# Two-block layer: stick-breaking attention summed by parts, and chunked attention's bias and maximum in one operation

## The chip, the cores and the metric

One core of one Trainium2 chip runs the program. The metric is the device time of one execution in microseconds (us). All data are float32. In the profile PE is TensorE (PEld its weight loads), DVE is VectorE, ACT is ScalarE, POOL is GpSimd and SP is the queue that issues weight loads.

## What is computed

The kernel computes two transformer blocks on 1024 rows of width 1024. Only a part of the second block is touched here: its two attentions, each with 8 heads of width 64.

```python
def chunked_attention(...):        # branch 0: a band of 9 chunks of 64 keys
    scores = einsum(q, k) * dh ** -0.5
    scores = where(valid, scores + bias, -inf)
    probs = softmax(scores, axis=-1)
    out = einsum(probs, v)

def stick_breaking_attention(q, k, v):   # branch 1: all keys before the query
    z = einsum(q, k) * dh ** -0.5
    log_keep = where(causal, -softplus(z), 0.0)
    log_after = cumsum(log_keep, reverse=True) - log_keep
    w = where(causal, exp(log_sigmoid(z) + log_after), 0.0)
    out = einsum(w, v)
```

In branch 1, softplus and log_sigmoid are never taken: keep = sigmoid(-z), take = sigmoid(z), left[j] is the product of keep from key j to the last key, and w[j] = take[j] * left[j+1].

## The kernel before, in words

The program is written out by hand for each engine: one Python function per engine and stage issues that engine's instructions in a fixed order, and semaphores (`mark` and `at`) tie the engines together. An engine never passes an instruction that waits. There is no scheduler.

The stage that matters is `att2`, from about 2075 to 2365 us. It has 64 units of work, `UNITS`: units 0 to 31 are branch 0 (4 pairs of heads, 8 query blocks of 128 rows each, t = 0 to 7) and units 32 to 63 are branch 1 (4 pairs, query blocks in the order t = 6, 7, 4, 5, 2, 3, 0, 1). A unit has two heads (hh = 0 and 1). In branch 0 a unit has 128 to 640 keys, in branch 1 it has 128 * (t + 1). Two units make a group g, whose values are summed at once. Every engine loops over u; in step u

- PE (`pe_att2`): scores of unit u + 2 (L3447, for branch 1 then the causal mask, L3456), the turning of unit u's weights, 128 x 128 blocks through PSUM banks 4 and 5 in turn (L3469), and half of the value sums of an earlier group (L3486). Scores over 512 keys take both PSUM banks of their head, so the next unit's scores must wait until all readers of them are done.
- ACT (`act_att2`): branch 0: exp with the maximum as bias (L3526); branch 1: keep (L3531) and take (L3533) from PSUM, for unit u + 2, head 0 before the copying of unit u's turned blocks to SBUF (L3544) and head 1 behind it. It also copies the output's high half (L3560).
- DVE (`dve_att2`): branch 0: scores plus bias (L3602), then their maximum (L3604), for unit u + 2; 1/sum (L3613); the output's scaling (L3639). Branch 1: the running product `left` of unit u + 1 (L3626), the copying of every second turned block group (L3635), and the output's low half (L3646). In branch 0 ACT copies all turned blocks.
- POOL (`pool_att2`): loads queries (L3681), keys and values of the next pair of heads (L3251, L3252; the values go to `v2`, as 8 blocks of 128 keys), biases; in branch 1 it multiplies take by the shifted left into w (L3702), which PE then turns.

`E2` has 6 slots of 1024 columns, a slot for each head of three units. `Sc` has 6 such slots too. Its first five are also `B`, the bias of branch 0; in branch 1 they hold take and w. In the first 6 units of branch 1 the scan's unused second operand is the scanned tile itself (SBUF), from then on a PSUM column.

Of the kernel before, what the change touches and what calls it, by code (L numbers as in the profile page):

```python
# [3420 lines left out]
def value_sums(g):  # L3421

    br, p, t = UNITS[2 * g]
    kbs = range(max(0, t - 4) if br == 0 else 0, t + 2)
    cols = {kb: slice(128 if kb > t else 0, 128 if br == 0 and kb == t - 4 else 256) for kb in kbs}
    return [(kb, cols[kb]) for kb in [t] + [kb for kb in kbs if kb != t]]


def pe_att2(k, e, free):
# [6 lines left out]
    def scores(u):  # L3436
# [5 lines left out]
        for a in range(0, n, 512):  # L3442
            w = min(512, n - a)
            for hh in range(2):
# [4 lines left out]
                free[b] = [s.dve.at("biased", u, hh) if br == 0 else s.act.at("take", u, hh)]  # L3449
# [64 lines left out]
def act_att2(k, e):  # L3514
    s, PS, H = k.att2, k.PS, k.H
    st, E, Sc = k.st2, k.E2, k.Sc

    def exponents(u, hh):
        br, p, t = UNITS[u]
        n, sl = span(br, t)[1], slot(u, hh)  # L3520
        if br == 0:
# [4 lines left out]
            e.activation(ev, ev, ACT.Exp, bias=st[:, sl, 0:1], accum_out=st[:, sl, 1:2]).then_inc(*s.act.mark("exp", u, hh))  # L3526
# [692 lines left out]
```

## Time and profile before

| | |
|---|---|
| median of 3 runs | 3213.13 us |
| lowest and highest run | 3210.9 and 3216.05 us |
| the profiled execution's own time | 3212.68 us |
| its span in the trace | 3210.8 us |
| PE, DVE, ACT, POOL busy, share of the span | 96%, 72%, 41%, 25% |

The profile shows the profiled execution alone. "Busy" counts every moment in which an instruction of the engine is shown; PE's ends are modelled and overlap, so its busy time is more than its work. Waits name who was waited for and for how long in all. A line such as L3604 is a line of the kernel before.

### The profile page before, as it was taken

How to read it: one execution, taken by the hardware profiler on the slowest of the kernel's cores; microseconds unless marked ns; L12 is line 12 of the kernel's file. 1: busy time of each engine (PE TensorE's matmuls, PEld its weight loads, DVE VectorE, ACT ScalarE, POOL GpSimd, SP SyncE). 2: the span in 40 equal slices, each digit the busy share in tenths (PEclk: the TensorE clock that was granted, in tenths of full speed). 3: DMA queues.
4: the chain of work that ended last, by engine and by line, in shares of the span. 5: the costliest groups of instructions: out<-in, count | busy, mean ns of one | idle time of the engine just before them, and what ended most of it. 6: DMA issues, size and time to landing. Idle time of an engine off the chain costs nothing.

```text
span 3210.8 us, 37676 instructions
## 1 busy us (share of the span) xinstructions
PE 3082.9 (96%) x14546; PEld 2417.3 (75%) x14546; DVE 2305.5 (72%) x3084; ACT 1303.1 (41%) x2124; POOL 807.8 (25%) x831
## 2 busy tenths in 40 slices
PE   7999998999999899999999999998899989999999
PEld 3577876777887788888877888764567877888787
DVE  6654456975657977778888566686644699899896
ACT  5431114761134433344454323476632344444443
POOL 1211101321120443320002444313533124333101
PEclk9999999999999999999999999999999999999999
DMA  6433352206743222246343346521123422222823
GB/s 223 156 133 132 136 206 102 80 14 236 266 142 116 99 86 86 80 150 226 112 135 112 97 124 202 174 99 39 39 89 113 156 86 85 79 85 73 298 89 112
DMA packets 118299, 406.86 MB, mean 127 GB/s; under 512 B 13704, under 2 KB 16328, under 8 KB 113642
## 3 DMA queue, kind: packets, MB, share of 16 engines
q1 hardware_dynamic: 65626, 200.42, 19.7%
q0 software_dynamic: 52496, 204.04, 17.7%
q8 instruction: 116, 1.90, 0.2%
q14 instruction: 61, 0.50, 0.0%
HBM read 321.50 MB, written 82.90 MB: 126 GB/s over the span
## 4 chain that ended last, share of the span: by engine, by line
PE 80%; DVE 11%; issue 3%; ACT 3%; DMA 2%; POOL 1%; SPq 0%; ACTq 0%; DVEq 0%; POOLq 0%
PE PS L455 23%; PE PS L457 23%; PE PS L456 23%; PE PS L1255 2%; PE PS L1295 2%; DVE HL L411 2%; PE PS L3447 2%; PE PS L1285 1%; PE PS L3469 1%; DMA RAW<-in_w_whyp 1%; POOL Sc L3702 1%; PE PS L3486 1%; ACT HL L393 1%; DVE Xp L1110 1%; DVE H L750 0%
## 5 line engine op out<-in xcount | busy, mean ns | idle before, releaser
L455 PE MATMUL PS<-H,HL 128*128 128x512 f32 x1920 | 761.1, 396 | 14.5 <-DVE H L3754 7.2
L456 PE MATMUL PS<-H,HL 128*128 128x512 f32 x1920 | 752.1, 392 | 0.0
L457 PE MATMUL PS<-H,HL 128*128 128x512 f32 x1920 | 752.0, 392 | 0.0
L393 ACT ACTIVATE HL<-RAW 128x512 fp32r<-128x512 f32 (+1 forms) x429 | 312.0, 728 | 619.6 <-PE PS L457 562.0
L411 DVE TENSOR_TENSOR HL<-RAW,HL 128x512 fp32r<-128x512 f32 (+1 forms) x429 | 400.1, 933 | 145.2 <-ACT HL L393 135.8
L455 PEld LDWEIGHTS PS<-H,HL 128*128 128x128 f32 x1920 | 363.2, 189 | 104.1 <-issue 19.3
L456 PEld LDWEIGHTS PS<-H,HL 128*128 128x128 f32 x1920 | 363.3, 189 | 76.9 <-issue 2.6
L457 PEld LDWEIGHTS PS<-H,HL 128*128 128x128 f32 x1920 | 363.1, 189 | 76.8
L455 PE MATMUL PS<-HT,HL 128*128 128x512 f32 x720 | 282.5, 392 | 17.8 <-DVE rows L2410 15.7
L456 PE MATMUL PS<-HT,HL 128*128 128x512 f32 x720 | 281.6, 391 | 0.0
L457 PE MATMUL PS<-HT,HL 128*128 128x512 f32 x720 | 281.4, 391 | 0.0
L393 ACT ACTIVATE HL<-SX 128x512 fp32r<-128x512 f32 x180 | 112.9, 629 | 247.5 <-PE PS L457 236.9
L455 PE MATMUL PS<-hsr,HL 128*128 128x512 f32 x464 | 182.1, 392 | 5.9 <-DVE hsr L2524 5.9
L456 PE MATMUL PS<-hsr,HL 128*128 128x512 f32 x464 | 181.3, 391 | 0.0
L457 PE MATMUL PS<-hsr,HL 128*128 128x512 f32 x464 | 181.2, 391 | 0.0
L455 PEld LDWEIGHTS PS<-HT,HL 128*128 128x128 f32 x720 | 136.1, 189 | 49.3 <-DVE HL L411 17.2
L457 PEld LDWEIGHTS PS<-HT,HL 128*128 128x128 f32 x720 | 136.0, 189 | 28.4
L456 PEld LDWEIGHTS PS<-HT,HL 128*128 128x128 f32 x720 | 136.2, 189 | 28.2
L411 DVE TENSOR_TENSOR HL<-SX,HL 128x512 fp32r<-128x512 f32 x180 | 134.5, 749 | 5.2 <-ACT HL L393 2.2
L328 POOL TENSOR_TENSOR SX<-RAW 128x512 f32<-128x512 f32 x56 | 73.8, 1319 | 243.6 <-DVE HL L411 205.9
L335 POOL TENSOR_TENSOR SX<-RAW,SX 128x512 f32<-128x512 f32 x56 | 105.1, 1877 | 96.4 <-DVE HL L411 96.4
L3447 PE MATMUL PS<-k,q 64*128 64x128 f32 (+3 forms) x384 | 95.3, 511 | 16.4 <-ACT Sc L3533 13.6
(465 smaller groups left out, 5633.0 us busy)
## 6 DMA issues: line engine op xcount, KB each, us to landing
RAW<-in_w_up SPq DMA_DIRECT2D x100, 512.0 KB, 3.6
RAW<-in_w_down SPq DMA_DIRECT2D x82, 512.0 KB, 3.8
RAW<-in_w_proj SPq DMA_DIRECT2D x48, 512.0 KB, 3.6
scr_hid<-hidr POOLq DMA_DIRECT2D x36, 512.0 KB, 2.9
RAW<-in_w_wmodr SPq DMA_DIRECT2D x32, 512.0 KB, 4.5
HL<-in_w_dfwd POOLq DMA_DIRECT2D x16, 1024.0 KB, 6.8
HL<-in_w_dinv POOLq DMA_DIRECT2D x16, 1024.0 KB, 5.4
RAW<-in_w_wout SPq DMA_DIRECT2D x26, 512.0 KB, 4.4
```

Of the source, the lines that this page charges most:

```text
L328: e.tensor_tensor(SX[:, 0, :], b[:, 0:512], b[:, 512:1024], ALU.add).then_inc(*signal.mark(j, "s1"))
L335: e.tensor_tensor(SX[:, 2, :], a[:, 512:1024], SX[:, 1, :], ALU.subtract).then_inc(*signal.mark(j, "s4"))
L393: e.activation(part_slot(k, p)[0], src, ACT.Copy).then_inc(*k.high.mark(j, x))
L411: e.tensor_tensor(lo, part_source(k, j, x)[0], hi.bitcast(F32), ALU.subtract).then_inc(*k.low.mark(j, x))
L455: e.matmul(out, lh, rh, start=first, stop=False, skip_group_check=goes_on)
L456: e.matmul(out, lh, rl, start=False, stop=False, skip_group_check=goes_on)
L457: return e.matmul(out, ll, rh, start=False, stop=last, skip_group_check=goes_on)
L1110: e.scalar_tensor_tensor(a, u, c, a, ALU.mult, ALU.add).then_inc(*s.dve.mark("mod", n))
L1255: x = e.matmul(k.PS[:, 3 * m + c, 0:b - a], k.q1[r, h % 2, blk(t)], k.k1[r, h % 2, a:b], start=True, stop=True)
L1285: x = e.transpose(PS[:, b, at + 128 * q:at + 128 * q + 128], weights_of(k, j, 0)[:, blk(4 * c + q)], k.ident[:, :])
L1295: x = e.matmul(PS[:, 7, 0:128], k.WT1[:, j % 2, kb, :], k.v1[:, j // 8 % 2, kb, :], start=(kb == 0), stop=(kb == 9))
L3447: x = e.matmul(PS[:, b, 0:w], k.q2[r, g % 2, blk(t % 2)], k.k2[r, pn % 2, lo * 128 + a:lo * 128 + a + w], start=True, stop=br == 0 or a + ...
```

## The change

1. **Branch 0, DVE.** The addition of the bias and the maximum are one operation, `tensor_tensor_reduce`, with -1 as a factor: E holds -(scores + bias), the reduction is a minimum, and ACT's exp takes scale -1. It is two instructions in the program, the operation and a read of its accumulator.
2. **Branch 0, copies.** Of a unit's turned block groups every second one is copied by DVE, as in branch 1 before.
3. **Branch 1, by parts.** take and w are gone. Since w[j] = left[j+1] - left[j], the output is the last row of v plus the sum over j of left[j] * (v[j-1] - v[j]). PE turns left out of `E2` at once. ACT makes only keep. POOL multiplies nothing.
4. **Branch 1, the steps of v.** For each pair of heads POOL sets one row to 0 (`load_steps`) and loads the values once more, shifted by one key: 127 partitions in one DMA, the 7 rows of partition 0 in another. DVE (`steps`) subtracts v from it in place (1024 columns) and then, in v's own place, adds v at partition 127 alone to the difference. This happens in step u = 30, 38, 46 and 54, ahead of the low half and the scans; the loads are issued in POOL's step u = 26, 34, 42 and 50, behind the keys and values of that pair. The place of the steps is slot 5 of `Sc`, or slot 0.
5. **Branch 1, value sums.** The diagonal key block's sum over 256 columns becomes two over 128, one with the changed v and one with the steps. All others take the steps. PE waits for `steps` ahead of the sums.
6. A bank of scores in branch 1 is free at keep, in branch 0 at the maximum.

```diff
-                unit.append((heads, c, w, 4 + n % 2, "dve" if br and len(unit) % 2 else "act"))
+                unit.append((heads, c, w, 4 + n % 2, "dve" if len(unit) % 2 else "act"))
...
 def value_sums(g):
...
+    if br:
+        left, right = slice(0, 128), slice(128, 256)
+        if t == 0:
+            return [(0, left, True, True, True), (0, right, False, True, False), (1, right, True, False, True)]
+        return ([(kb, slice(0, 256), False, kb == 0, False) for kb in range(t)]
+                + [(t, left, True, False, True), (t, right, False, False, False), (t + 1, right, True, False, True)])
...
+def v_steps(k, p):
+    return k.Sc[:, 5 * (1 - p % 2), :].rearrange("p (t n) -> p t n", t=8)
...
-                free[b] = [s.dve.at("biased", u, hh) if br == 0 else s.act.at("take", u, hh)]
+                free[b] = [s.dve.at("max", u, hh) if br == 0 else s.act.at("keep", u, hh)]
...
-                e.wait_ge(*(s.act.at("exp", u, hh) if br == 0 else s.pool.at("w", u, hh)))
-                src = k.E2 if br == 0 else k.Sc
+                e.wait_ge(*(s.act.at("exp", u, hh) if br == 0 else s.dve.at("left", u, hh)))
...
+            if br:
+                e.wait_ge(*s.dve.at("steps", p, 1))
...
-        for i, (kb, cols) in list(enumerate(sums))[m * half:m + m * half]:
+        for kb, cols, whole, first, last in sums[m:] if half else sums[:m]:
+            v = k.v2[:, pn % 2] if whole else v_steps(k, p)
...
-        e.wait_ge(*s.dve.at("biased", NU // 2 - 1, 1))
-        e.activation(Sc[:, sl, 0:n], z, ACT.Sigmoid).then_inc(*s.act.mark("take", u, hh))
...
-        e.tensor_tensor(ev, scores_of(k, u, hh), B[:, 2 * p + hh, 640 - n:640], ALU.add).then_inc(*s.dve.mark("biased", u, hh))
-        e.wait_ge(*s.dve.at("biased", u, hh))
-        e.tensor_reduce(st[:, sl, 0:1], ev, AX.X, ALU.max, negate=True).then_inc(*s.dve.mark("max", u, hh))
+        e.tensor_tensor_reduce(ev, scores_of(k, u, hh), B[:, 2 * p + hh, 640 - n:640], -1.0, 3.0e38, ALU.add, ALU.min,
+                               st[:, sl, 0:1]).then_inc(*s.dve.mark("max", u, hh))
...
+    def steps(p):
+        v, d = k.v2[:, p % 2], v_steps(k, p)
+        e.wait_ge(*k.in_pair[p % 2].at(4 + p, 1))
+        e.wait_ge(*k.in_steps[p % 2].at(p, 1))
+        e.wait_ge(*s.pool.at("first", p))
+        e.tensor_tensor(d, d, v, ALU.subtract).then_inc(*s.dve.mark("steps", p, 0))
+        e.wait_ge(*s.dve.at("steps", p, 0))
+        e.scalar_tensor_tensor(v, v, k.ident[:, 127:128], d, ALU.mult, ALU.add).then_inc(*s.dve.mark("steps", p, 1))
...
+def load_steps(k, e, p):
+    s, d, src = k.att2, v_steps(k, p), k.d_v2[1][:, :, blk(p)].rearrange("t p n -> p t n")
+    if p == 1:
+        e.wait_ge(*s.dve.at("max", NU // 2 - 1, 1))
+    at = k.in_steps[p % 2]
+    e.memset(d[0:1, 0, :], 0.0).then_inc(*s.pool.mark("first", p))
+    e.dma_start(d[1:128], src[0:127]).then_inc(*at.mark(p, 0))
+    e.dma_start(d[0:1, 1:8], src[127:128, 0:7]).then_inc(*at.mark(p, 1))
...
-        if u + 1 < NU and UNITS[u + 1][0] == 1:
-            n = span(1, UNITS[u + 1][2])[1]
-            for hh in range(2):
-                sl = slot(u + 1, hh)
-                tk = Sc[:, sl, 0:n - 1]
-                e.wait_ge(*s.dve.at("left", u + 1, hh))
-                e.wait_ge(*s.act.at("take", u + 1, hh))
-                e.tensor_tensor(tk, tk, E[:, sl, 1:n], ALU.mult).then_inc(*s.pool.mark("w", u + 1, hh))
+            if u // 8 + 1 >= 4:
+                load_steps(k, e, u // 8 - 3)
```

Where instructions move, three places show it; a tile's name there ends in a number that means nothing (`E_121` is `E2`, `v_119` is `v2`). First ACT, in branch 1, from the last step of one pair of heads to the first long units (896 and 1024 keys) of the next. Before:

```order
L3531 ACTIVATE E_121<-PS 128x896
L3533 ACTIVATE Sc_120<-PS 128x896
L3531 ACTIVATE E_121<-PS 128x1024
L3533 ACTIVATE Sc_120<-PS 128x1024
L3544 ACTIVATE WT_122<-PS 128x2x2x128
L3531 ACTIVATE E_121<-PS 128x1024
L3533 ACTIVATE Sc_120<-PS 128x1024
L3560 ACTIVATE H<-PS 128x256
```

And of the change:

```order
L3544 ACTIVATE E_121<-PS 128x896
L3544 ACTIVATE E_121<-PS 128x1024
L3555 ACTIVATE WT_122<-PS 128x2x2x128
L3544 ACTIVATE E_121<-PS 128x1024
L3571 ACTIVATE H<-PS 128x256
```

Each keep stands alone; the takes into `Sc` behind them are gone, and nothing else has moved on ACT here.

Second DVE in branch 0, one step with 640 keys (`Rb` is the scaled output). Before:

```order
L3602 TENSOR_TENSOR E_121<-PS,Sc_120 128x640
L3604 TENSOR_REDUCE st_127<-E_121 128x1
L3602 TENSOR_TENSOR E_121<-PS,Sc_120 128x640
L3604 TENSOR_REDUCE st_127<-E_121 128x1
L3639 TENSOR_TENSOR Rb_125<-PS,Rb_125 128x256
```

And of the change:

```order
L3613 ISA E_121,st_127<-PS,Sc_120 128x640
L3613 ISA st_127 128x1
L3613 ISA E_121,st_127<-PS,Sc_120 128x640
L3613 ISA st_127 128x1
L3655 COPY WT_122<-PS 128x4x128
L3659 TENSOR_TENSOR Rb_125<-PS,Rb_125 128x256
```

The two reductions have become two short accumulator reads, and a copy that was ACT's stands ahead of the scaling.

Third POOL, from the loads of the next pair of heads on. Before:

```order
L3251 DMA k_118<-scr_qk 128x1024
L3252 DMA v_119<-scr_v 128x8x128
L3702 TENSOR_TENSOR Sc_120<-Sc_120,E_121 128x767 x2
L3702 TENSOR_TENSOR Sc_120<-Sc_120,E_121 128x383 x2
L3681 DMA q_117<-scr_qk 128x256
```

And of the change:

```order
L3251 DMA k_118<-scr_qk 128x1024
L3252 DMA v_119<-scr_v 128x8x128
L3712 MEMSET Sc_120 1x128
L3713 DMA Sc_120<-scr_v 127x8x128
L3714 DMA Sc_120<-scr_v 1x7x128
L3703 DMA q_117<-scr_qk 128x256 x4
```

The multiplications are gone, and POOL's queue holds only loads: three more instructions stand behind the values of each pair.

## Rows read from the trace of the kernel before

**Rows 1.** Stretches: length, PE, PEld, DVE, ACT, POOL busy (instructions), PE clock, DMA share, GB/s.

```profile
2084.84:2185.04 100.20, 99.80 (x745) 61.82 (x745) 86.59 (x203) 77.26 (x204) 13.40 (x23) 1.00 0.29 100
2185.04:2205.05 20.01, 14.84 (x74) 8.48 (x74) 5.12 (x7) 14.84 (x21) 5.66 (x3) 0.74 0.02 7
2205.05:2239.04 33.99, 27.74 (x200) 17.78 (x200) 29.32 (x28) 17.61 (x40) 17.77 (x18) 0.95 0.12 41
2239.04:2251.11 12.07, 8.97 (x44) 4.19 (x44) 5.54 (x5) 8.16 (x11) 4.94 (x5) 0.98 0.06 17
2251.11:2279.61 28.50, 25.74 (x175) 15.93 (x176) 21.07 (x25) 16.78 (x37) 17.62 (x18) 0.95 0.15 50
2279.61:2319.87 40.26, 35.07 (x219) 20.41 (x218) 26.62 (x29) 24.93 (x48) 22.57 (x23) 0.96 0.12 39
2319.87:2357.47 37.60, 31.79 (x208) 18.65 (x207) 25.06 (x26) 24.44 (x47) 19.38 (x18) 1.00 0.03 10
2357.47:2365.20 7.73, 5.96 (x40) 3.74 (x39) 2.44 (x5) 2.13 (x5) 1.65 (x4) 1.00 0.01 2
```

**Rows 2.** Waits, chunked half, 2084.84 to 2185.04 us: total us, times, longest.

```profile
PEld PS L3447 <- DVE E L3602: 6.0, 13, 1.1
...
PEld PS L3469 <- ACT WT L3544: 3.7, 10, 0.4
```

**Rows 3.** Groups of instructions, chunked half, 2075 to 2186 us.

```profile
L3604 DVE TENSOR_REDUCE st<-E 128x1 f32<-128x640 f32 (+4 forms) x64 | 41.8, 654 | 2.2
L3602 DVE TENSOR_TENSOR E<-PS,Sc 128x640 f32<-128x640 f32 (+4 forms) x64 | 41.5, 648 | 1.1 <-PE PS L3447 0.6
```

**Rows 4.** Groups by form, whole run: the fused operation of the first block, line 1463.

```profile
L1463 DVE CUSTOM_DVE_ANT_0 E<-PS,st 128x1280 f32<-128x1280 f32 x54 | 78.7, 1488 | 18.7 <-PE PS L1255 18.7
...
L1463 DVE DVE_READ_ACCUMULATOR2_ANT st<- 128x1 f32 x64 | 5.3, 83 | 0.0
```

**Rows 5.** Groups, one full pair of heads, 2239.04 to 2279.61 us.

```profile
L3626 DVE TENSOR_TENSOR_SCAN E<-E,PS 128x256 f32<-128x256 f32 (+7 forms) x17 | 21.8, 1299 | 0.9 <-ACT E L3531 0.9
...
L3635 DVE COPY WT<-PS 128x512 f32<-128x512 f32 (+1 forms) x8 | 5.2, 644 | 5.2 <-PE PS L3469 5.2
```

**Rows 6.** Timeline, second long unit of a pair: start us, us, instruction.

```profile
2285.29 0.44 PE L3456 MATMUL PS<-maskr,identr 128*128 128x128 f32 x2
...
2285.65 1.02 ACT L3531 ACTIVATE E<-PS 128x1024 f32<-128x1024 f32 x1 [2.33 <-PE PS L3456]
...
2286.57 1.02 ACT L3533 ACTIVATE Sc<-PS 128x1024 f32<-128x1024 f32 x1
2287.47 0.60 ACT L3544 ACTIVATE WT<-PS 128x512 f32<-128x512 f32 x1
...
2288.85 1.06 ACT L3533 ACTIVATE Sc<-PS 128x1024 f32<-128x1024 f32 x1
...
2291.24 0.44 PE L3456 MATMUL PS<-maskr,identr 128*128 128x128 f32 x2
```

**Rows 7.** Groups by form, whole run: scans with and without a PSUM operand.

```profile
L3626 DVE TENSOR_TENSOR_SCAN E<-E 128x1024 f32<-128x1024 f32 x2 | 6.0, 3004 | 0.0
...
L3626 DVE TENSOR_TENSOR_SCAN E<-E,PS 128x1024 f32<-128x1024 f32 x6 | 13.7, 2276 | 0.0
```

**Rows 8.** Groups by form, whole run: VectorE operations like those that are added.

```profile
L411 DVE TENSOR_TENSOR HL<-RAW,HL 128x1024 fp32r<-128x1024 f32 x103 | 132.1, 1284 | 109.4 <-ACT HL L393 102.0 <-ACT acc2r L1932 7.4
...
L2816 DVE SCALAR_TENSOR_TENSOR HTf<-HTf,gsc,RR 128x512 f32<-128x512 f32 x16 | 11.6, 747 | 0.1
L1971 DVE SCALAR_TENSOR_TENSOR HTf<-HTf,gsc,PS 128x512 f32<-128x512 f32 x16 | 11.5, 741 | 1.2 <-PE PS L1920 1.2
```

**Rows 9.** DMA, while a pair's values land, 2263.9 to 2265.4 us: packets; queue's engine share; issues.

```profile
DMA packets 104, 0.37 MB, mean 249 GB/s; under 512 B 13, under 2 KB 13, under 8 KB 104
...
q0 software_dynamic: 104, 0.37, 87.6%
...
v<-scr_v POOLq DMA_DIRECT2D x1, 512.0 KB, 5.7
```

More of the change, by code:

```diff
@@ L3423, in value_sums @@
     br, p, t = UNITS[2 * g]
-    kbs = range(max(0, t - 4) if br == 0 else 0, t + 2)
-    cols = {kb: slice(128 if kb > t else 0, 128 if br == 0 and kb == t - 4 else 256) for kb in kbs}
-    return [(kb, cols[kb]) for kb in [t] + [kb for kb in kbs if kb != t]]
+    if br:
[4 more added lines that the diff above has]
+                + [(t, left, True, False, True), (t, right, False, False, False), (t + 1, right, True, False, True)])
+    kbs = range(max(0, t - 4), t + 2)
+    cols = {kb: slice(128 if kb > t else 0, 128 if kb == t - 4 else 256) for kb in kbs}
+    order = [t] + [kb for kb in kbs if kb != t]
+    return [(kb, cols[kb], True, kb == t, kb == order[-1]) for kb in order]
+def v_steps(k, p):
+    return k.Sc[:, 5 * (1 - p % 2), :].rearrange("p (t n) -> p t n", t=8)
 def pe_att2(k, e, free):
@@ L3465, in turn @@
             for i, hh in enumerate(heads):
-                e.wait_ge(*(s.act.at("exp", u, hh) if br == 0 else s.pool.at("w", u, hh)))
-                src = k.E2 if br == 0 else k.Sc
+                e.wait_ge(*(s.act.at("exp", u, hh) if br == 0 else s.dve.at("left", u, hh)))
                 for q in range(w):
-                    y = e.transpose(PS[:, b, blk(w * i + q)], src[:, slot(u, hh), blk(c + q)], k.ident[:, :])
+                    y = e.transpose(PS[:, b, blk(w * i + q)], k.E2[:, slot(u, hh), blk(c + q)], k.ident[:, :])
             y.then_inc(*s.pe.mark("turn", u, x))
@@ L3481, in values_of @@
                     e.wait_ge(*turned(k, u, x))
+            if br:
+                e.wait_ge(*s.dve.at("steps", p, 1))
             claim(b)
-        for i, (kb, cols) in list(enumerate(sums))[m * half:m + m * half]:
+        for kb, cols, whole, first, last in sums[m:] if half else sums[:m]:
+            v = k.v2[:, pn % 2] if whole else v_steps(k, p)
             for hh in range(2):
                 r = slice(64 * hh, 64 * hh + 64)
-                x = e.matmul(PS[r, b, cols], k.v2[:, pn % 2, kb, r], k.WT2[:, g % 2, hh, kb, cols], start=(i == 0), stop=(i == 2 * m - 1),
-                             skip_group_check=True)
+                x = e.matmul(PS[r, b, cols], v[:, kb, r], k.WT2[:, g % 2, hh, kb, cols], start=first, stop=last, skip_group_check=True)
         if half == 0:
@@ L3515, in act_att2 @@
     s, PS, H = k.att2, k.PS, k.H
-    st, E, Sc = k.st2, k.E2, k.Sc
+    st, E = k.st2, k.E2
     def exponents(u, hh):
@@ L3525, in exponents @@
                 e.wait_ge(*s.dve.at("inv", u - 3))
-            e.activation(ev, ev, ACT.Exp, bias=st[:, sl, 0:1], accum_out=st[:, sl, 1:2]).then_inc(*s.act.mark("exp", u, hh))
+            e.activation(ev, ev, ACT.Exp, bias=st[:, sl, 0:1], scale=-1.0, accum_out=st[:, sl, 1:2]).then_inc(*s.act.mark("exp", u, hh))
             return
@@ L3658, in dve_att2 @@
                 biased(u + 2, hh)
+        if u >= NU // 2 - 2 and u % 8 == 6 and u // 8 - 3 < 4:
+            steps(u // 8 - 3)
         scan = u + 1 < NU and UNITS[u + 1][0] == 1
@@ L3681, in load_queries @@
     e.dma_start(k.q2[:, g % 2, :], k.d_qk2[8 * br + p][:, blk(t // 2, 256)]).then_inc(*k.in_q[g % 2].mark(g))
+def load_steps(k, e, p):
[6 more added lines that the diff above has]
+    e.dma_start(d[0:1, 1:8], src[127:128, 0:7]).then_inc(*at.mark(p, 1))
 def pool_att2(k, e):
-    s, E, Sc = k.att2, k.E2, k.Sc
     for u in range(NU + 2):
@@ L3912, in build @@
         k.in_q = [dma(f"in_q{i}") for i in range(2)]
+        k.in_steps = [dma(f"in_steps{i}") for i in range(2)]
         k.in_gate = [dma(f"in_gate{i}") for i in range(4)]
```

## The prediction

> **What bounds the kernel now.** I first cut the stage in stretches by the moment at which PE first turns a block of a unit, and read who is busy in each [rows 1]. The reader is to see two halves of one stage that have different limits. In the chunked half PE shows 99.8 us of 100.2; DVE (86.6) and ACT (77.3) have little room. In the stick-breaking half (2205 to 2365 us) nobody is full: PE shows 27.7 of 34.0 us, then 34.7 of 40.6 (8.97 and 25.74 of 12.07 and 28.50), and DVE 26.6 of the same 40.6. So the second half is a chain from engine to engine, and what shortens the chain shortens the kernel. What follows the stage starts when it ends, on data that are already there, so I count each microsecond saved in it in full; outside it nothing changes.
>
> Second, the waits of the chunked half: weight loads wait 6.0 us for DVE's additions before scores and 3.7 us for ACT's copies before turning [rows 2]. PE's own row hides these, because its ends overlap.
>
> Third, the timeline where a pair of heads begins, the stretch of 12.07 us [rows 6]. Its unit has 1024 keys, hence both score banks of each head. From mask (2285.29) to mask (2291.24) there are 5.95 us, and they are ACT's: keep, take, a copy, keep, take, and only then PE's next scores. A take costs 0.90 us from its start to the next start (2286.57 to 2287.47).
>
> **The change, part by part.** The sum is made against the profiled execution, 3212.68 us, which is 0.45 us below the median of the runs.
>
> *Chunked half.* Gone from DVE: 64 reductions at 654 ns, 41.8 us [rows 3]. Added: 64 accumulator reads at 83 ns, 5.3 us; the fused operation itself I price from the same operation in the first block, 1280 columns in 1488 ns [rows 4]. At 640 columns that is 0.74 us if it is halved and 0.87 us on the line through the 747 ns that a two-input operation takes at 512 columns [rows 8]; either way it is what an addition costs now (648 ns in the mean over all sizes [rows 3]), so it takes the addition's place at no cost. Added too are 24 copies (one a unit for t = 2 to 7, 4 pairs) at about 644 ns [rows 5], 15.5 us. DVE falls by 41.8 - 5.3 - 15.5 = 21 us, ACT by some 14. But PE shows 99.8 of 100.2 us, so the gain is only what PE waits for. From below it is 0 (PE was full). From above it is twice the 9.7 us of weight-load waits for DVE and ACT [rows 2], since a late head also breaks the pairing of the two heads' scores on PE; but the pairing I can't price, and I cut this at 14. A bank of scores is freed 0.08 us later for head 0 than today, yet some 0.6 us sooner for head 1, which no longer waits for head 0's reduction. I take **-7**.
>
> *The switch between the halves*, 20.0 us with PE at a mean clock of 0.74, that is for a part at 1.2 GHz. ACT is the chain here: two tables swapped, four takes of about 0.9 us before the next scores are in, and two copies. The takes leave (3.6 us) and a copy or two goes to an idle DVE; but PE's own work behind them, partly at the low clock, stays. Ends -1 and -6; I take **-3**.
>
> *First pair of the second half*, 33.99 us, DVE 29.3 busy. Here scans read SBUF twice while POOL multiplies: 1024 columns take 3004 ns against 2276 with a PSUM operand [rows 7]. POOL stops multiplying, so ten scans lose up to 0.73 us each; I take 5 us off DVE, leaving 24, and PE's 27.7 sets the end: **-7** (ends -5 and -8).
>
> *Two full pairs*, 40.57 and 40.26 us. The opening 12.07 us hold two such links; each loses two takes, so 4 x 0.9 = 3.5 us: 8.6 remain. In the other 28.5 us the multiplication on POOL between scan and turning is gone, and the takes too; what is late next is DVE, in order: scan, copy, scan, copy. DVE has 26.6 us a pair and gets the steps: 1.28 us for the subtraction, between 1.28 and 2 x 0.75 us for the other [rows 8], so 2.6, in all 29.2. PE's shown 25.7 of 28.5 has overlaps in it, so I let these 28.5 become 25. Each pair then takes 33.6: **-14** for both. Ends: -8 (the opening links and a little) and -20 (DVE's 29.2 plus one us).
>
> The second operation of the steps reads two SBUF tiles. In this trace such an operation takes 747 ns at 512 columns against 741 with one operand in PSUM [rows 8], so two SBUF inputs cost nothing extra. The Trainium skill says otherwise (Vector Engine (DVE) Microarchitecture Reference, section Points that are easy to get wrong): this form with two SBUF sources that are not bf16 runs at half the throughput. By that rule the sum would be up to 4 us higher; the row decides.
>
> *Last pair*, 37.60 us: the same less the next pair's scores, **-6** (ends -4 and -8). *Tail*, 7.73 us: two waits for POOL's product go, **-0.7**.
>
> *At nothing:* the split of the diagonal value sum (32 matmuls more, each half as wide as the one it replaces, so the same columns); exp's factor; POOL's added issues, which stand in a queue that waits most of the time; the steps' DMA, if it lands like the values, 5.7 us after its issue [rows 9], four steps (about 16 us) ahead of its use. If that cover is gone, DVE stops, with all scans and copies behind it: see the second rival.
>
> Sum: 7 + 3 + 7 + 14 + 6 + 0.7 = 37.7; 3212.7 - 37.7 = **3175**.
>
> **Rivals.**
> 1. *PE is the bound all along.* Its 99.8 of 100.2 us and 34.7 of 40.6 are real work, so only the takes on the chain count. Chunked 0, switch -1, pairs -5, -8, -4: 3212.7 - 18 = 3195. For: PE's rows. Against: it waits for ACT and POOL in the stick half, and its shown ends overlap. Chance 0.12.
> 2. *The shifted load is slow* (the other side). Values land as packets of 4 KB, one a partition: 91 of them and 13 small ones fill 87.6% of 16 engines for 1.5 us, so 0.23 us a packet [rows 9]; 128 over 16 engines are quick. 127 partitions don't divide by 16. If they all go to one DMA engine, that is 127 x 0.23 = 29 us. For pairs 2 to 4 the load is issued just over a microsecond after the first turning of the third unit of the pair before and `steps` is due some 16 us after that turning: DVE would stand 15 to 16 us in each, 47 in all, and at the first pair some 5 more beyond what it idles anyway. 3175 + 52 = 3227. It decides for slower once the stops pass 38 us in all, some 11 a pair. For: no load in this trace has such a shape, so nothing here excludes it. Against: an engine that cuts 127 rows in 8 a piece is as fast as now. Chance 0.13. The Trainium skill (DMA: Bandwidth & Descriptors, section Why a DMA increments its semaphore by 16 and not by 1) states both: the engine count must divide the slowest dimension, so 127 partitions use one, but some direct copies issued from GpSimd are spread over all 16 with 8 partitions each.
> 3. *The fusion does not fuse.* In the first block its second tensor is one broadcast value; with a full bias tile it may need two passes, 1.49 us at 640 columns. DVE keeps its 41.8 us and gets the reads and copies on top, 107 us in the 100-us half: +7 there in place of -7, so 3189. Chance 0.05.
>
> **How the numbers follow.** The forecast (3157 to 3195 with all ends at once) gets 0.66, rival 1 0.12, rival 2 0.13, rival 3 0.05, and 0.04 is for what I don't see, most of it near no change. Some 0.2% (6.4 us) can be told from no change. Faster: 0.66 + 0.12 + 0.05 = 0.83; same 0.03; slower 0.14. The range, 3157 to 3198, takes in the forecast's ends and rivals 1 and 3, and leaves rival 2 out.
>
> **What would show it.** DVE's fused row near 0.8 us at 640 columns and no reduction; about 94 us for the stretch that is 100.2 now; mask to mask at 4.1 to 4.2 us where it is 5.95; scans of 1024 columns at 2.28 us from the first pair on; a full pair at 33 to 34 us with DVE above 85% busy; the steps' load landing within 10 us. I am wrong if DVE's longest wait is for a DMA, if a pair still takes 37 us or more, or if the chunked half has not moved.

## The result, and the profile after

The changed kernel takes **3286.18 us** (median of 4 runs, 3283.45 to 3287.46) where before takes 3212.02 beside it (3210.03 to 3216.05): ratio 1.0228, 95% interval [1.021, 1.0246]. It is slower by some 73 us. The prediction was 3175, faster. Of the variants below, one execution of e5 (4671.46 us), the first of e7 (3978.16) and one of before beside them (5130.09) came in a slow state: the medians count them (without it e5's is 3164.20), the ratios and all readings of profiles leave them out.

Cut at the same moments as before [rows 1] (the first turning of units 2, 28, 30, 32, 38, 46, 54, 62; units 2 to 30 together here), the changed kernel's stage reads:

```profile
2080.16:2165.34 85.18, 85.06 (x685) 54.53 (x683) 58.29 (x206) 61.40 (x168) 12.77 (x22) 1.00 0.34 115
2165.34:2205.01 39.67, 10.15 (x64) 5.96 (x63) 7.99 (x18) 7.15 (x17) 8.38 (x4) 0.62 0.11 22
2205.01:2221.01 16.00, 13.94 (x73) 8.33 (x74) 6.52 (x9) 9.68 (x14) 0.54 (x1) 0.77 0.03 9
2221.01:2274.98 53.97, 27.40 (x208) 17.72 (x208) 25.29 (x30) 12.78 (x28) 10.52 (x8) 0.77 0.15 38
2274.98:2336.37 61.39, 34.48 (x233) 20.63 (x234) 28.82 (x30) 16.71 (x32) 11.04 (x9) 0.75 0.14 36
2336.37:2397.92 61.55, 34.51 (x233) 20.63 (x234) 28.82 (x30) 16.71 (x32) 11.05 (x9) 0.75 0.14 36
2397.92:2428.81 30.89, 30.62 (x223) 18.89 (x224) 24.80 (x25) 16.33 (x31) 1.07 (x2) 0.96 0.03 9
```

The rows hold gains and losses at once. The chunked half up to unit 28 is 85.18 us where before has 91.91 (100.20 of [rows 1] less the 8.29 of units 28 and 29), and the last pair is 30.89 for 37.60. But the pair of units from 2165.34 takes 39.67 us for 8.29, and each of the next three pairs of heads is 20 to 21 us longer than before. There are four such places, one for each load of the steps. The longest waits of 2160 to 2440 us name it (engine, what waits, for whom: total us, times, longest; the first row is ScalarE behind the stopped TensorE):

```profile
ACT E L3544 <- PE PS L3468: 159.0, 28, 30.5
PEld PS L3459 <- issue: 126.1, 68, 29.7
POOL q L3703 <- issue: 104.4, 4, 26.5
DVE Sc L3633 <- issue: 96.5, 4, 25.3
...
PE PS L3459 <- DMA q<-scr_qk: 79.7, 3, 26.8
PE PS L3459 <- issue: 29.5, 1, 29.5
...
POOL Sc L3713 <- issue: 20.2, 4, 5.6
```

Line 3713 is the load of 127 partitions, 3703 the load of queries, 3633 the subtraction of the steps, 3459 the scores. Three engines stop at each of the four places, for up to 25 to 30 us. POOL's timeline at the first of them (start us, us, instruction, idle before it) shows the order of things:

```profile
2158.91 0.90 POOL L3252 DMA_DIRECT2D v<-scr_v  x1
2159.80 0.20 POOL L3712 MEMSET Sc<- 1x128 f32 x1
2165.55 6.71 POOL L3713 DMA_DIRECT2D Sc<-scr_v  x1 [5.56 <-issue]
2172.26 0.55 POOL L3714 DMA_DIRECT2D Sc<-scr_v  x1
2198.57 1.13 POOL L3703 DMA_DIRECT2D q<-scr_qk  x2 [25.77 <-issue]
```

The values' load takes 0.90 us to issue. The shifted one waits 5.56 us for nothing that the profile shows and then takes 6.71 us, and the queries behind it go out 25.77 us after the one-row load. DVE and PE at the same place:

```profile
2172.82 0.22 DVE L3623 RECIPROCAL rr<-st 128x1 f32<-128x1 f32 x2
2198.32 1.22 DVE L3633 TENSOR_TENSOR Sc<-Sc,v 128x1024 f32<-128x1024 f32 x1 [25.28 <-issue]
```

```profile
2171.28 0.44 PE L3480 MATMUL PS<-ident,E 128*128 128x128 f32 x2
2201.24 3.36 PE L3459 MATMUL PS<-k,q 64*128 64x512 f32 x8 [29.52 <-issue]
```

DVE goes on at 2198.32, POOL at 2198.57, and PE one queries' load later. So all three are released by one moment, the end of the two loads of the steps: 26.0 us after the one-row load was issued, and 32.8 us after the issue of line 3713 began. (The trace gives 3713 itself a landing of 21.7 us; it shares its semaphore with the next load, and its packets go on to 2197.5, so I don't use that figure. Where e3 gives it a semaphore of its own it lands after 32.4 to 33.0 us.) What moves meanwhile, 2165 to 2199 us:

```profile
DMA packets 2081, 0.60 MB, mean 18 GB/s; under 512 B 1946, under 2 KB 1953, under 8 KB 2080
```

At a pair's values it is 249 GB/s [rows 9]. The data are 127 packets of 4 KB. In the trace's list each takes 192 ns and 5 or 6 start in every microsecond from 2173 to 2197.5 us, one after another: 127 x 0.192 = 24.4 us. That is the work of one DMA engine; the trace does not name the engine, so this is read from the pace. Beside them stand 1905 packets of 32 bytes and 15 ns, 15 a partition. They do not set the pace: the last starts at 2188.1 us, and the large ones go on as before. (In the whole run 21489 packets are under 512 B, against 13768 in the variant e1 below, which has no such load: 7721 more for four.)

The operations themselves came as priced:

```profile
L3613 DVE CUSTOM_DVE_ANT_0 E<-PS,Sc 128x640 f32<-128x640 f32 x32 | 25.1, 822 | 5.9 <-PE PS L3459 5.4
...
L3646 DVE TENSOR_TENSOR_SCAN E<-E,PS 128x1024 f32<-128x1024 f32 x6 | 13.7, 2275 | 0.0
...
L3613 DVE DVE_READ_ACCUMULATOR2_ANT st<- 128x1 f32 x64 | 5.3, 83 | 0.0
...
L3635 DVE SCALAR_TENSOR_TENSOR v<-v,ident,Sc 128x1024 f32<-128x1024 f32 x4 | 5.1, 1285 | 0.1
...
L3633 DVE TENSOR_TENSOR Sc<-Sc,v 128x1024 f32<-128x1024 f32 x4 | 4.9, 1225 | 96.5 <-issue 96.5
```

The fused operation takes 0.82 us at 640 columns; the steps take 1.23 and 1.29 us. The only new thing in these rows is the last one's idle time. The second step reads two SBUF tiles in 1285 ns, within the 1.28 to 2 x 0.75 us of the prediction, and under twice the 741 ns of an operation at 512 columns with one source in PSUM [rows 8]; the Trainium skill's rule that was weighed there (Vector Engine (DVE) Microarchitecture Reference, section Points that are easy to get wrong), by which it would run at half the throughput, is not borne out here.

### The profile page after: what moved, and what is told of

It is laid out like the page before. It is cut to its first block, busy times and chain, and to the rows that moved or that the text cites. A ratio compares the mean times of both kernels' runs of the same rounds, so it can differ in the third digit from the quotient of the medians.

```text
span 3281.6 us, 37598 instructions
## 1 busy us (share of the span) xinstructions
PE 3072.7 (94%) x14610; PEld 2414.6 (74%) x14610; DVE 2283.8 (70%) x3116; ACT 1259.8 (38%) x2036; POOL 760.4 (23%) x779
## 2 busy tenths in 40 slices
DMA packets 126619, 409.20 MB, mean 125 GB/s; under 512 B 21489, under 2 KB 24141, under 8 KB 121963
## 4 chain that ended last, share of the span: by engine, by line
PE 81%; DVE 10%; issue 5%; ACT 2%; DMA 2%; SPq 0%; POOL 0%; DVEq 0%; ACTq 0%; POOLq 0%
PE PS L455 22%; PE PS L456 22%; PE PS L457 22%; PE PS L1255 2%; PE PS L3459 2%; PE PS L1295 2%; PE PS L3500 2%; PE PS L3480 2%; DVE HL L411 2%; PE PS L1285 1%; DMA RAW<-in_w_whyp 1%; ACT HL L393 1%; DVE Xp L1110 1%; DVE H L750 0%; PE PS L3103 0%
## 5 line engine op out<-in xcount | busy, mean ns | idle before, releaser
L3459 PEld LDWEIGHTS PS<-k,q 64*128 64x128 f32 x384 | 37.5, 200 | 149.7 <-issue 138.5
```

What stands on the lines that cost most here:

```text
L3459: x = e.matmul(PS[:, b, 0:w], k.q2[r, g % 2, blk(t % 2)], k.k2[r, pn % 2, lo * 128 + a:lo * 128 + a + w], start=True, stop=br == 0 or a + ...
```

## The experiments

Eleven kernels, one of them run twice. Beside each stands the kernel before, timed on the same chip: 3211.89 us for e1 to e4, 3209.37 for e5 to e8, 3209.81 for the rest. The intervals of the ratios reach 3 to 6 us to either side, so the terms are read from each kernel's own profiled execution, in the same stretches (us; the first is units 2 to 30, "sum" ends at the first turning of unit 62):

| kernel | time | ratio to before | chunked | switch | first pair | 2nd | 3rd | last | sum |
|---|---|---|---|---|---|---|---|---|---|
| before | | | 100.20 | 20.01 | 33.99 | 40.57 | 40.26 | 37.60 | 272.6 |
| changed | 3286.18 | 1.0228 | 124.85 | 16.00 | 53.97 | 61.39 | 61.55 | 30.89 | 348.7 |
| e1 | 3166.74 | 0.9862 | 93.18 | 16.81 | 25.85 | 32.61 | 32.62 | 30.63 | 231.7 |
| e2 | 3169.07 | 0.9869 | 93.17 | 16.81 | 25.85 | 32.62 | 32.61 | 30.64 | 231.7 |
| e3 | 3260.14 | 1.0153 | 93.17 | 16.81 | 56.42 | 62.54 | 63.09 | 30.57 | 322.6 |
| e4 | 3202.92 | 0.9967 | 93.17 | 16.81 | 25.86 | 32.61 | 49.98 | 47.16 | 265.6 |
| e5 | 3166.09 | 0.9863 | 93.18 | 17.87 | 25.86 | 32.61 | 32.61 | 30.64 | 232.8 |
| e6 | 3183.31 | 0.9914 | 107.86 | 16.71 | 25.86 | 32.62 | 32.61 | 30.64 | 246.3 |
| e7, 2nd run | 3189.81 | 0.9937 | 93.18 | 18.55 | 25.94 | 37.97 | 39.57 | 35.40 | 250.6 |
| e8 | 3204.38 | 0.9984 | 93.17 | 19.94 | 34.00 | 40.10 | 41.77 | 38.11 | 267.1 |
| e9 | 3176.34 | 0.9896 | 93.42 | 16.86 | 30.78 | 32.62 | 32.61 | 30.64 | 236.9 |
| e10 | 3266.41 | 1.0174 | 93.17 | 34.60 | 25.86 | 58.61 | 58.72 | 56.21 | 327.2 |
| e11 | 3190.99 | 0.9940 | 93.45 | 16.87 | 37.23 | 36.64 | 36.78 | 34.07 | 255.0 |

What stands around the stage varies by more than the terms. From unit 62 to the end of the span there are 852.6 (e5) to 855.7 us (e8); 853.3 before, 852.8 changed, 853.4 in e1. And the stage's first turning, of unit 0, comes at 2070.3 (e5) to 2080.0 us (e10), though the program ahead of the stage is the same. So whole times differ by some us for reasons outside the stage: e1 is 45 us below before by its time and 41 by its stage.

### The load: e1 and e2

**e1** loads all 128 partitions from one row earlier of the scratch tensor, in one piece; the first row, which is then a stray one, is zeroed behind it.

```diff
-    e.memset(d[0:1, 0, :], 0.0).then_inc(*s.pool.mark("first", p))
-    e.dma_start(d[1:128], src[0:127]).then_inc(*at.mark(p, 0))
-    e.dma_start(d[0:1, 1:8], src[127:128, 0:7]).then_inc(*at.mark(p, 1))
+    rows = k.d_v2[:, :, :, :].rearrange("a t p n -> (a t p) n")[1023:2047, blk(p)].rearrange("(t p) n -> p t n", t=8)
+    e.dma_start(d, rows).then_inc(*at.mark(p, 1))
...
-        e.wait_ge(*s.pool.at("first", p))
+        e.memset(d[0:1, 0, :], 0.0).then_inc(*s.dve.mark("first", p))
+        e.wait_ge(*s.dve.at("first", p))
```

> The steps' values are loaded by one transfer of 128 partitions (it starts one row earlier in the scratch; DVE zeroes the one wrong row) in place of 127 and 1. Theory A (the 127-row load runs on one DMA engine, some 24 us of packets, and everything that waits behind it makes the loss): landing near 6 us, no wait of DVE for it, no long pause on POOL, the kernel at 3170 to 3180 us, as the sum of the prediction had it. Rival B (the loss is not the shape: the additional loads or the wait for the steps cost whatever their shape): the kernel stays above 3260 us.

3166.74 us (3163.79 to 3170.79), ratio 0.9862 [0.9848, 0.9877], 3 us below the range that I expected. POOL's timeline, and behind it the DMA issues of 2160 to 2320 us (what, how many, KB each, us to landing):

```profile
2157.78 0.90 POOL L3252 DMA_DIRECT2D v<-scr_v  x1
2158.67 0.89 POOL L3714 DMA_DIRECT2D Sc<-scr_v  x1
2161.48 0.56 POOL L3704 DMA_DIRECT2D q<-scr_qk  x1 [1.92 <-PE PS L3459]
```

```profile
v<-scr_v POOLq DMA_DIRECT2D x3, 512.0 KB, 5.9
Sc<-scr_v POOLq DMA_DIRECT2D x3, 512.0 KB, 6.5
```

Same bytes, same queue, same place: 0.89 us to issue and 6.5 us to land, like the values. No pause stands before the queries. This one edit is worth 119 us (3286.18 less 3166.74), and the rest of the change is a gain of 45 (41 in the stage).

**e2** keeps the destination and its 127 partitions and cuts them in 112 and 15.

```diff
-    e.dma_start(d[1:128], src[0:127]).then_inc(*at.mark(p, 0))
+    e.dma_start(d[1:113], src[0:112]).then_inc(*at.mark(p, 0))
+    e.dma_start(d[113:128], src[112:127]).then_inc(*at.mark(p, 2))
```

> The changed kernel, but the 127 rows are loaded as 112 and 15. If the number of DMA engines must divide the number of partitions, these take 16 and 15 engines, and the time is that of e1 plus at most 2 us for one more issue a pair. If instead only full 128-partition loads are spread, both are slow and the kernel stays near 3286 us. Theory B also says near 3286 us.

3169.07 us, ratio 0.9869, 2.3 us from e1, and the same stretches as e1 to 0.02 us. The groups of POOL and the landings:

```profile
L3713 POOL DMA_DIRECT2D Sc<-scr_v x4 | 3.4, 847 | 0.0
L3714 POOL DMA_DIRECT2D Sc<-scr_v x4 | 2.4, 601 | 0.0
L3715 POOL DMA_DIRECT2D Sc<-scr_v x4 | 2.1, 536 | 0.0
```

```profile
Sc<-scr_v POOLq DMA_DIRECT2D x4, 448.0 KB, 5.9
Sc<-scr_v POOLq DMA_DIRECT2D x4, 60.0 KB, 5.5
Sc<-scr_v POOLq DMA_DIRECT2D x4, 3.5 KB, 5.8
```

So it is neither the shift by a partition, nor the odd start, nor the small load behind it: it is that one load has 127 partitions. Numbers other than 127, 112, 15 and 128 were not tried. Of the two statements of the Trainium skill that the prediction cited (DMA: Bandwidth & Descriptors, section Why a DMA increments its semaphore by 16 and not by 1), the rule is what the trace shows (127 has no divisor up to 16 but 1, and its packets keep one engine's pace; 112 = 16 x 7 and 15 are fast), and the exception for direct copies from GpSimd did not hold for this load.

### Who pays for it: e3, e10 and e4

**e3** is e1, and for pairs 2 to 4 POOL also issues the slow load to a slot that nobody reads, and nobody waits for it in the stage.

```diff
     e.dma_start(d, rows).then_inc(*at.mark(p, 1))
+    if p:
+        x = k.Sc[:, p, :].rearrange("p (t n) -> p t n", t=8)
+        e.dma_start(x[1:128], src[0:127]).then_inc(*k.in_waste.mark(p))
```

> e1, and for three of the four pairs the 127-row load is issued too, at its old place in POOL's queue, into a slot that nobody reads, and nobody waits for it before the stage's end. Theory Q (the loss comes by POOL's queue: the next queries can't be issued while the slow load runs, and PE waits for them): three stalls of 25 to 30 us on PE, 3250 to 3265 us. Theory D (the loss comes by DVE's wait for the steps, as the prediction's second rival had it): no stall, 3175 us or less.

3260.14 us, ratio 1.0153 (e1: 0.9862); the three stretches lose 30.6, 29.9 and 30.5 us. DVE's steps wait for nothing. What waits, 2160 to 2440 us:

```profile
...
PEld PS L3459 <- issue: 102.0, 70, 29.0
...
PE PS L3459 <- DMA q<-scr_qk: 85.3, 3, 28.8
...
POOL q L3704 <- issue: 78.9, 3, 26.6
```

A load that nobody needs costs 30 us, because the queries stand behind it in POOL's queue and PE stands behind the queries.

**e10** is the other half: the changed kernel with its slow load as it is, but from unit 28 the queries are issued by SyncE's queue.

```diff
+    for g in range(14, NG):
+        load_queries(k, e, g)
...
-        if u % 2 == 0 and u // 2 + 2 < NG:
+        if u % 2 == 0 and u // 2 + 2 < 14:
             load_queries(k, e, u // 2 + 2)
```

> The changed kernel with its slow load as it is, but the stick-breaking half's queries issued by SyncE's queue instead of GpSimd's, so that nothing waits behind the load but the reader of the steps. Theory Q (the loss is the queries' wait behind the load in GpSimd's queue): TensorE's waits for queries vanish and what is left is VectorE's stop for the steps, landing about 28 us after the first issue against 16 us of cover, so 10 to 16 us in each of four pairs: 3167 + 40 to 60 = 3207 to 3227. Rival R (the packets of 32 bytes slow everything that moves in these 25 us): the queries land late from this queue too, and it stays above 3270.

3266.41 us (3264.72 to 3268.1), ratio 1.0174: only 20 us better than the changed kernel (3286.18), and far above the 3207 to 3227 that I expected. PE's waits for queries are gone, as expected; DVE's are all there:

```profile
...
DVE Sc L3635 <- issue: 98.4, 4, 25.5
...
PEld PS L3502 <- DVE H L3668: 76.8, 8, 25.4
```

So both stops last nearly the whole 25 to 30 us by themselves, and in the changed kernel they lie side by side: DVE alone costs 95.5 us in the sum of the stretches (e10 against e1, four loads, 24 each), the queries alone 30 a load (e3), both 117.0 for four, 29 each. The rival expectation, that the packets slow whatever moves, fails too: the queries from SyncE's queue are in time.

**e4** is e1's kernel with the slow loads issued by SyncE's queue, and the queries left on POOL's.

```diff
+    for p in range(4):
+        load_steps(k, e, p)
...
+    if p >= 2:
+        e.wait_ge(*s.pe.at("pv", 4 * (p + 2) + 3))
...
-            if u // 8 + 1 >= 4:
-                load_steps(k, e, u // 8 - 3)
```

> The changed kernel's 127-row and 1-row loads, but issued from SP's queue and so not ahead of the queries; DVE zeroes the row. Landing then is all that counts. Theory Q: PE's waits for queries go; what is left is DVE's wait for pairs 3 and 4 (the first two can be loaded long ahead), 5 to 10 us each: 3180 to 3195 us. Theory D: DVE's waits stay as long as the load takes, above 3220 us. If SP's loads were spread over engines where POOL's are not, 3170 to 3180 us.

3202.92 us, ratio 0.9967 (e1: 0.9862), above the upper end of what I expected. The first two loads go out early and cost nothing; the other two have to wait for the pair before and cost 17.4 and 16.5 us. Its waits, and then SyncE's two issues of the last pair (start us, us):

```profile
...
PEld PS L3502 <- DVE H L3669: 34.0, 8, 15.8
...
DVE Sc L3634 <- DMA Sc<-scr_v: 29.6, 2, 14.9
```

```profile
2282.12 0.23 SPq L3717 DMA_DIRECT2D Sc<-scr_v  x1
2282.40 26.86 SPq L3718 DMA_DIRECT2D Sc<-scr_v  x1
```

The issue is 0.24 us here, but the transfer is no faster for it: it moves in packets of 512 B, 27 ns each and some 42 started in a microsecond, again about one engine's work, and the 1016 of them take 27 us. DVE stops 14.9 us. This is the size that my second rival had for a stop, but not for its reason alone: from the first issue to DVE's release there are 31.1 us (2282.12 to 2313.25) where POOL's way takes 38.5, and DVE comes 16.2 us behind the issue where it comes 14.5 us behind on POOL's way (last pair of heads; the terms stand below).

### What the rest is worth: e5, e6, e8 (chunked half)

**e5** is e1 with the chunked half's copies all on ACT again; **e6** is e1 with addition and reduction apart; **e8** is the kernel before with the fused operation and the shared copies alone.

```diff
-                unit.append((heads, c, w, 4 + n % 2, "dve" if len(unit) % 2 else "act"))
+                unit.append((heads, c, w, 4 + n % 2, "dve" if br and len(unit) % 2 else "act"))
```

```diff
-        e.tensor_tensor_reduce(ev, scores_of(k, u, hh), B[:, 2 * p + hh, 640 - n:640], -1.0, 3.0e38, ALU.add, ALU.min,
-                               st[:, sl, 0:1]).then_inc(*s.dve.mark("max", u, hh))
+        e.tensor_tensor(ev, scores_of(k, u, hh), B[:, 2 * p + hh, 640 - n:640], ALU.add).then_inc(*s.dve.mark("biased", u, hh))
+        e.wait_ge(*s.dve.at("biased", u, hh))
+        e.tensor_reduce(st[:, sl, 0:1], ev, AX.X, ALU.max, negate=True).then_inc(*s.dve.mark("max", u, hh))
```

> e1 with the chunked half's turned-block copies all on ScalarE again (24 copies of about 0.64 us leave VectorE). Theory 'the fused operation earned the chunked half's 6.7 us': the stretch from the transposes of unit 2 to those of unit 28 stays within 2 us of e1's 84.9, total 3167 to 3169. Rival 'the copies earned it': the stretch goes back towards 91.9 and the total towards 3173.

> e1 with the addition and the reduction apart again, the copies still shared. VectorE gets 64 x (654 - 83) ns = 36.5 us in a stretch where it was 58 of 85 us busy, so it nears 90% and its two heads come 0.65 us apart again. Theory 'the fused operation earned it': the stretch of units 2 to 28 back to 91 to 93 us, total 3172 to 3176. Rival 'the copies earned it': 85 to 86 us, total within 2 us of e1's 3167.

> The kernel before with the chunked half's part alone: the fused operation and the shared copies, nothing of the stick-breaking half changed (so no shifted load either). If the parts add, the chunked half gives 6 to 8 us and the total is 3204 to 3206. If the gain is given back at the switch between the halves, where the stick-breaking half then starts from the same place earlier, it is 3210 to 3212.

e5: 3166.09 us, ratio 0.9863 [0.9844, 0.9881], and the chunked stretch is 93.18 as in e1, as expected. The copies on VectorE give nothing there; they take 1.06 us off the switch. e6: 3183.31 us, ratio 0.9914 [0.99, 0.9928], and the chunked stretch is 107.86 us, 7.7 *above* before, where I expected at most the old pace. The two stretches, e5 first:

```profile
2075.89:2169.07 93.18, 93.18 (x747) 59.63 (x745) 51.47 (x202) 77.14 (x205) 14.59 (x24) 1.00 0.34 114
```

```profile
2084.46:2192.32 107.86, 103.95 (x745) 62.88 (x745) 98.07 (x226) 68.30 (x182) 14.36 (x24) 1.00 0.29 98
```

In e6 VectorE (third busy column) is at 98.07 of 107.86 us: with two operations a head it has no room for copies. In e5 it has 51.47. The whole 7 us are the fused operation's, and it alone makes the shared copies bearable. e8: 3204.38 us, ratio 0.9984 [0.9975, 0.9993]; its chunked stretch is e1's, 7.03 us below before, and its stick-breaking half is before's but for one pair that is 1.5 us longer. The part stands by itself, as expected.

### What the rest is worth: e7, e11 and e9 (stick-breaking half)

The change took two things from between scores and turning. **e7** is e1 with the take back on ACT, written to slots that nobody reads, the banks freed by it; **e11** is e1 with a product on GpSimd between scan and turning, of the same size as before's, its result unread.

```diff
-                free[b] = [s.dve.at("max", u, hh) if br == 0 else s.act.at("keep", u, hh)]
+                free[b] = [s.dve.at("max", u, hh) if br == 0 else s.act.at("take", u, hh)]
...
+        e.wait_ge(*s.dve.at("max", NU // 2 - 1, 1))
+        e.activation(k.Sc[:, 1 + (2 * u + hh) % 4, 0:n], z, ACT.Sigmoid).then_inc(*s.act.mark("take", u, hh))
```

```diff
-                e.wait_ge(*(s.act.at("exp", u, hh) if br == 0 else s.dve.at("left", u, hh)))
+                e.wait_ge(*(s.act.at("exp", u, hh) if br == 0 else s.pool.at("w", u, hh)))
...
+                e.tensor_tensor(k.Sc[:, 1 + (2 * u + hh) % 4, 0:n - 1], k.E2[:, sl, 0:n - 1], k.E2[:, sl, 1:n], ALU.mult).then_inc(*k.att2.pool.mark("w", u + 1, hh))
```

> e1 with the second sigmoid (the take) back on ScalarE, written to slots that nobody reads, and the score banks freed by it as before; GpSimd's product stays away. This splits the stick-breaking half's gain. Theory L 'the takes on the chain at the pair's opening': each opening (a unit of 1024 keys and the one after) loses 3.6 us again, so a pair takes about 36 us where e1 has 32.6 and before had 40.4, total 3167 + 4 x 3.5 = about 3181 to 3184. Rival M 'the chain was GpSimd's product': a pair stays within 1 us of 32.6 and the total is under 3172. Rival N 'all of it was the takes': a pair of 39 to 40 us, total about 3200.

> e7 once more, to have its profile at the clock of the others (the time of the first, 3191, is 26 us above e1). By the time, a pair of heads should take about 39 us where e1 has 32.6; if the loss is at the pair's opening link alone, the unit pair with 1024 keys takes 3.6 us more than e1's 8.44 and the rest is unchanged, which would make only 3.6 of the 6.5 us a pair. So I expect the other three pairs of units to be longer too, by 1 us each.

> e1 with a product on GpSimd between scan and transposes again (of the scanned rows with their neighbours, written where nobody reads), and no take on ScalarE. The take alone costs 26 us (e7), the whole half gained about 38 in the stage. Theory 'take and product lie on one chain and their costs add': 12 us, 3 a pair, total 3177 to 3180. Rival 'each alone is enough to set the old pace': 25 to 38 us, total 3192 to 3204.

e7: 3191.22 us the first time, 3189.81, ratio 0.9937 [0.9924, 0.9951], the second, whose profile is the one read here; both are above the 3181 to 3184 that I expected. e11: 3190.99, ratio 0.9940 [0.9927, 0.9952], just under the 3192 to 3204 of its rival expectation, that each alone sets the old pace. By the stretches they give back 18.9 and 23.3 us, together 42.2, where the whole half, switch and pairs, gained 33.9 (172.4 before, 138.5 in e1). So each alone sets part of the old pace, and they are partly alternatives. The second pair of heads of each, e7 first:

```profile
2221.51:2259.48 37.97, 34.32 (x234) 21.32 (x234) 29.05 (x32) 24.94 (x48) 4.50 (x7) 0.96 0.18 57
```

```profile
2225.95:2262.59 36.64, 33.05 (x234) 19.84 (x234) 27.97 (x30) 16.74 (x32) 22.52 (x23) 1.00 0.18 57
```

By pairs of units the two are complements. In e7 the opening 8.45 us of e1 become 12.11 and the next 8.28 become 9.98, the other two stay (8.52, 7.36); in the third pair of heads they are 12.45 and 11.24, at a mean clock of 0.91. In e11 the opening stays (8.45) and the others become 9.51, 10.20 and 8.48. So the take is the opening's, the product that of the shorter units, as the prediction split them; my expectation for e7, that the other units get longer by 1 us each, was wrong for two of three. In the first pair the take costs nothing (25.94) and the product 11.4 us (37.23). Of these, 6.3 us are ten scans with both sources in SBUF that run longer beside GpSimd (1024 columns: 2946 ns for 2283); the clock there is 0.86 for 1.00, and the rest was not separated.

**e9** is e1 with the steps computed on GpSimd, as three operations, so that VectorE loses 2.4 us a pair.

```diff
-                e.wait_ge(*s.dve.at("steps", p, 1))
+                e.wait_ge(*s.pool.at("steps", p, 2))
...
+        e.tensor_tensor(d, d, v, ALU.subtract).then_inc(*s.pool.mark("steps", p, 0))
+        e.wait_ge(*s.pool.at("steps", p, 0))
+        e.tensor_tensor(v, v, k.ident[:, 127:128].to_broadcast([128, 8, 128]), ALU.mult).then_inc(*s.pool.mark("steps", p, 1))
+        e.wait_ge(*s.pool.at("steps", p, 1))
+        e.tensor_tensor(v, v, d, ALU.add).then_inc(*s.pool.mark("steps", p, 2))
```

> e1 with the steps of the values taken on GpSimd (subtraction, product with the last row's mark, addition) in place of VectorE, eight units ahead of their use. VectorE is busy 28.8 of 32.6 us a pair and loses 2.5 us of it. Theory 'VectorE sets the pair': 1.5 to 2.5 us less a pair, total 3158 to 3162. Rival 'TensorE sets it (31.7 of 32.6 us busy)': within 1 us a pair, total 3165 to 3168. Rival 'GpSimd's operations slow VectorE's scans or hold up a queries' load': slower than e1.

3176.34 us, ratio 0.9896 [0.9883, 0.991], slower than e1. A full pair is 32.62 us as in e1, though VectorE is busy 26.41 instead of 28.84: VectorE does not set it, and the steps cost nothing on VectorE once their load is in time. TensorE is busy 32.34 of 32.62, so it is the likely bound, but this is not shown: its ends are modelled, and in the chunked half a row as full hid 7 us. The stage's loss is mostly in the first pair, 4.9 us, where two scans of 512 columns that run beside GpSimd's operations are 3.0 us longer (groups by form, e9 and then e1):

```profile
L3636 DVE TENSOR_TENSOR_SCAN E<-E 128x512 f32<-128x512 f32 x2 | 5.4, 2714 | 0.0
```

```profile
L3647 DVE TENSOR_TENSOR_SCAN E<-E 128x1024 f32<-128x1024 f32 x2 | 4.6, 2283 | 0.0
...
L3647 DVE TENSOR_TENSOR_SCAN E<-E 128x512 f32<-128x512 f32 x2 | 2.4, 1215 | 0.0
```

e1's stage is the shortest of all that ran, with e2's: the kernel is 1.4% below before, 3.6% below the changed kernel.

## Why the prediction was wrong

**The step that failed** is in the part *At nothing*: "the steps' DMA, if it lands like the values, 5.7 us after its issue". It does not: 39.4 us pass from the values' issue (2158.91) to the first operation on the steps (2198.32). The prediction had the mechanism as its second rival, gave it 0.13 and left it out of the range.

**The rival's own sum was half of what the runs showed**, 52 us against 95.5 for DVE's stops alone (e10 against e1). Its terms, for one stop:

- Transfer: 127 x 0.23 = 29 us. Measured 127 x 0.192 = 24.4 us. It is about right.
- Issue: not priced. Measured at the first place 5.56 us before and 6.71 us of issuing, 12.3 us in which nothing of it moves. This is the larger error. e4, where the issue takes 0.24 us, stops for 14.9 us in the last pair, 9.0 less than the 24.0 here: 7.3 by the shorter way to the release, 1.7 by the longer cover.
- Cover: 16 us from the third unit's turning, so just under 15 from the issue. Measured from the end of the values' issue to DVE at the steps: 14.5 us in pairs 2 to 4, and 13.2 at the first (2159.81 to 2173.04). It is about right.
- Sum: 12.3 + 24.4 is 36.7, and 38.5 pass from 2159.81 to 2198.32. Less 13.2 of cover that is 25.3 us; at the other three places, with 14.5 of cover, the stops are 23.5, 23.8 and 24.0 us. The first pair, for which I took 5, is no exception.

**The queue behind it was not asked about.** "POOL's added issues ... stand in a queue that waits most of the time" was priced at nothing. Behind them stand the queries, held up for 25.8 us. This costs 30 us a load where nobody waits for the load itself (e3), and beside DVE's stop another 21.5 us for all four in the sum of the stretches (117.0 less 95.5). The rival's rule for the sign ("slower once the stops pass 38 us in all") was right: 117 less 41 is 76 in the stage, and 73 were measured.

**The sum of gains was right, term by term.** With the load made harmless (e1), against the predicted terms: chunked -7.0 (predicted -7), switch -3.2 (-3), first pair -8.1 (-7), two full pairs -15.6 (-14), last pair -7.0 (-6), together -40.9 (-37.0); the tail's -0.7 is not to be seen. A pair takes 32.6 us for the predicted 33.6, with VectorE at 28.84 of it, 88% (predicted above 85%). From mask to mask at a pair's second long unit, predicted 4.1 to 4.2 us, e1's timeline has 4.11:

```profile
2251.84 0.44 PE L3468 MATMUL PS<-maskr,identr 128*128 128x128 f32 x2
...
2252.20 1.02 ACT L3544 ACTIVATE E<-PS 128x1024 f32<-128x1024 f32 x1 [2.33 <-PE PS L3468]
...
2253.60 1.03 ACT L3544 ACTIVATE E<-PS 128x1024 f32<-128x1024 f32 x1
...
2255.95 0.44 PE L3468 MATMUL PS<-maskr,identr 128*128 128x128 f32 x2
```

Rival 1 (TensorE the bound all along) is answered in two parts: in the chunked half its full row hid 7 us of waiting, as I took it; after the change it may be the bound of a pair, which e9 fits but does not show. Rival 3 falls: 0.82 us at 640 columns is one pass. The chunked term was right in size but its reason was half wrong: I gave the copies a share, and they have none (e5). The two full pairs came out right partly by luck: I took VectorE for what is late next, and e9 takes 2.4 us a pair off it without moving the pair by more than 0.01 us.

The profile's clue was there: no load before has 127 partitions, and so nothing in the trace priced this one. The prediction said so and still entered the load at nothing; the range should have reached at least the 3227 of its own rival.

## What to carry to other kernels

Before a load is priced like its neighbour, count its partitions: 112 + 15 landed in 6 us, 127 in 33. Starting one row earlier for a round 128 took 0.9 us of POOL's time to issue, the split with its one-row load 2.0, and the stage was as long with either. A DMA has three prices, and each has its own victims: the time that the issuing engine spends (whatever is next in that queue), the transfer, and the reader's stop, which is what the cover does not reach. A step whose cover is 13 to 15 us and whose price is unknown belongs in the range, whatever its chance.

## What the runs showed of the hardware

- A load of 127 partitions (4 KB each) issued by GpSimd: a pause of 4.6 to 5.6 us, 6.7 us of issuing (0.9 for 128), 24.4 us of 4 KB packets one after another, at one DMA engine's pace, and 1905 packets of 32 bytes beside them. GpSimd's next load but one went out only when it had ended; what holds it there was not tried. Issued by SyncE it takes 0.24 us to issue and moves as 1016 packets of 512 B in 27 us, no faster.
- A scan with both sources in SBUF costs no more than one with a PSUM source while GpSimd is idle, 2283 ns at 1024 columns (e1) against 2275; beside GpSimd's product it takes 2946 (e11) to 3004 ns [rows 7], and at 512 columns beside GpSimd's steps 2714 ns (e9) for 1215. The Trainium skill names the place (GPSIMD Engine Reference, section 1. Specifications: GpSimd's access to SBUF is shared with VectorE, with contention for instructions with two SBUF inputs), and the trace agrees: two such scans are 3.0 us longer in e9, ten are 6.3 us longer in e11. How much of this the stage pays was not separated.
- The 25 us stops lower TensorE's clock: its mean granted clock is 0.75 to 0.77 in the changed kernel's pairs and 1.00 in e1's, so part of the work after a stop ran at the lower level, 1.2 GHz, and the same 234 matmuls of a pair show 34.5 us busy for 31.7. So by estimate some 3 us a pair (34.5 less 31.7) of the loss come with the stop and not in it.
